# The products with w_in_2 as three fp32r products of rounded and remaining parts, their weights in panels of half a slot

## What is computed

```python
u = modulate(rmsnorm(h, norm_mix_g), shift, scale)      # 512 x 1024
z, xbc, dt_raw, xp, gates = split(u @ w_in_2)           # z 2048, xbc 4096, dt 32, pool 1024, gates 2048 columns
y_ssd  = ssd_branch(z, xbc, dt_raw, ...)                # conv, silu, chunked state-space scan: 8 groups x 4 chunks of 128
y_pool = pool_branch(xp, pool_w, pool_scale)            # window means, a grouped product
h = h + mod * ((y_ssd @ w_br_ssd) * sigmoid(g0) + (y_pool @ w_br_pool) * sigmoid(g1)) @ w_out_2
# then router, 64 experts (top 8), shared expert, final norm
```

## Time and profile before

| | |
|---|---|
| median of 3 runs | 2885.08 us (2883.0 to 2885.61) |
| the profiled execution | 2896.94 us, span 2894.9 us |
| PE busy | 2614.2 us (90%) of the span |
| DVE, ACT, POOL busy | 1111.9, 655.1, 538.1 us |
| mean granted TensorE clock | 0.928 |

### The profile page before, as it was taken

One profiled execution on the slowest core, in us unless ns is written; L12 is line 12 of the kernel. 1 busy time (PEld: TensorE's weight loads), 2 busy tenths in 40 slices (PEclk: granted clock), 3 DMA queues, 4 the chain that ended last, 5 costly groups with the idle time before them and its releaser, 6 DMA issues.

```text
span 2894.9 us, 25467 instructions
## 1 busy us (share of the span) xinstructions
PE 2614.2 (90%) x8938; PEld 1524.9 (53%) x8938; DVE 1111.9 (38%) x2005; ACT 655.1 (23%) x1084; POOL 538.1 (19%) x442
## 2 busy tenths in 40 slices
PE   5999996899999889999998899986889999999995
PEld 3885345678777533445454444574444444444443
DVE  4545333499851332445555321124611111111113
ACT  3334243333332222222222110222111111111111
POOL 2330003234333200000000001130322322222220
PEclk8997678899999899899999799997989999999998
DMA  3222000155632022211112011212089999999995
GB/s 117 75 88 87 1 0 30 58 175 181 214 122 102 0 87 83 66 44 44 56 46 87 30 58 58 87 33 80 31 324 304 343 339 314 353 331 332 324 321 147
DMA packets 163575, 403.43 MB, mean 139 GB/s; under 512 B 12128, under 2 KB 88928, under 8 KB 139552
## 3 DMA queue, kind: packets, MB, share of 16 engines
q1 hardware_dynamic: 142896, 342.27, 33.2%
q0 software_dynamic: 19440, 55.79, 8.0%
q10 hardware_dynamic: 1152, 4.19, 0.4%
HBM read 378.62 MB, written 39.32 MB: 144 GB/s over the span
## 4 chain that ended last, share of the span: by engine, by line
PE 78%; DVE 9%; DMA 7%; issue 2%; ACT 2%; POOL 1%; POOLq 0%; SPq 0%; DVEq 0%; ACTq 0%
PE bank L644 42%; PE bank L653 19%; DMA arena<-u_rows,rows_in 4%; PE bank L811 3%; PE bank L751 2%; PE bank L728 2%; PE bank L1078 2%; PE bank L670 2%; PE bank L918 1%; DVE hn L1594 1%; DMA arena<-in_w_up 1%; PE bank L742 1%; DVE arena L1725 1%; PE bank L732 1%; DVE inv L1591 1%
## 5 line engine op out<-in xcount | busy, mean ns | idle before, releaser
L644 PE MATMUL bank<-arena 128*128 128x512 f32 x1840 | 812.6, 598 | 8.6 <-DVE arena L1940 5.8
L644 PEld LDWEIGHTS bank<-arena 128*128 128x128 f32 x1840 | 348.2, 192 | 421.2 <-issue 417.1
L644 PE MATMUL bank<-hn,arena 128*128 128x512 f32 (+1 forms) x1168 | 530.8, 614 | 13.7 <-ACT hn L1161 10.6
L644 PEld LDWEIGHTS bank<-hn,arena 128*128 128x128 f32 (+1 forms) x1168 | 225.2, 195 | 298.7 <-issue 282.5
L2060 DVE TENSOR_TENSOR arena<-arena,bank 128x256 f32<-128x256 f32 x62 | 26.1, 421 | 501.6 <-ACT arena L1554 501.6
L603 POOL DMA_INDIRECT y_rows<-arena,rows_out x62 | 98.8, 1594 | 504.8 <-DVE arena L2072 271.2
L653 PE MATMUL bank<-x_high,w_high 128*128 128x512 f32 x352 | 141.1, 401 | 14.1 <-DVE x_low L1601 13.0
L560 POOL TENSOR_TENSOR pooled_low<-arena,pooled_high 128x512 fp32r<-128x512 f32 x8 | 9.9, 1266 | 742.8 <-ACT pooled_high L1473 742.8
L653 PE MATMUL bank<-x_low,w_high 128*128 128x512 f32 x352 | 139.7, 397 | 0.0
L653 PE MATMUL bank<-x_high,w_low 128*128 128x512 f32 x352 | 139.7, 397 | 0.0
L2072 DVE TENSOR_SCALAR arena<-bank,arena 128x512 f32<-128x512 f32 x124 | 93.1, 751 | 115.8 <-PE bank L644 115.8
(11 more groups left out here) (307 smaller groups left out, 3919.1 us busy)
## 6 DMA issues: line engine op xcount, KB each, us to landing
arena<-in_we_gate SPq DMA_DIRECT2D x62, 1024.0 KB
arena<-in_we_up SPq DMA_DIRECT2D x62, 1024.0 KB
arena<-in_we_down SPq DMA_DIRECT2D x62, 1024.0 KB, 8.7
arena<-in_w_in SPq DMA_DIRECT2D x30, 1024.0 KB, 5.9
arena<-in_w_ada SPq DMA_DIRECT2D x12, 2048.0 KB, 8.1
arena<-in_w_up SPq DMA_DIRECT2D x22, 1024.0 KB, 11.3
arena<-in_w_in SPq DMA_DIRECT2D x17, 512.0 KB, 4.2
arena<-in_w_out SPq DMA_DIRECT2D x4, 2048.0 KB, 8.1
```

The source lines that it names most:

```text
L644: ins = nc.tensor.matmul(out, w(k), rhs(k), start=first and k == 0, stop=last and k == nk - 1)
```

## The change

Each of the 73 products becomes a `split_product`. ACT makes the activations' high parts straight from the scaled norm (adding the shift), DVE the low parts, for which `hn` no longer holds the shifted sum. Weights come in panels of half a slot (8 x 256 columns): four half-slots in slots 0 and 1, and slot 2 holds the high parts of two panels in turn. Such a panel with its one or two tiles is a unit. ACT rounds unit u+2 as soon as it has read the last product of unit u (`in2_high_part`), POOL subtracts tile by tile into the panel's own place, and PE waits for its tile's low part. The squares of the group norm move from `sq` to another buffer.

```diff
@@ panels
-        x_panel = len(PANELS)
-        for c0, c1, v in ((6144, 6560, 4), (6560, 6944, 7), (6944, 7200, 9)):
-            add_panel(one(w_in2, 0, KD, c0, c1), S("product"), PRODUCTS["x"] + v)
+        def add_half_panel(copies, value):
+            n = len(IN2)
+            IN2.append(add_panel(copies, S("product"), value, NSLOT + n % 4, [latest[n // 2]] if n < 4 else [IN2[n - 4]]))
+        for c0, c1, v in ((6144, 6304, 2), (6304, 6560, 4), (6560, 6816, 6), (6816, 6944, 7), (6944, 7200, 9)):
+            add_half_panel(one(w_in2, 0, KD, c0, c1), PRODUCTS["x"] + v)
...
+        last = {s: [i for i in IN2 if SLOT_OF[i] == NSLOT + s][-1] for s in range(4)}
+        FREED = {0: [last[0], last[1]], 1: [last[2], last[3]], 2: [IN2[-1]]}
...
                 add_panel(one(A["w_br_ssd"], KD * kg, KD * kg + KD, 512 * half, 512 * half + 512),
-                          S("product"), PRODUCTS["ssd_out"] + 2 * half + kg + 1)
+                          S("product"), PRODUCTS["ssd_out"] + n + 1, n % NSLOT, FREED[n] if n < NSLOT else None)
@@ POOL
+            for j, (u, i) in enumerate(IN2_TILES):
+                pool_eng.wait_ge(S("w_high"), W_UNITS["in2"] + u + 1)
+                pool_eng.tensor_tensor(in2_tile(j, "low"), in2_tile(j, "whole"), in2_tile(j, "high").bitcast(f32),
+                                       ALU.subtract).then_inc(S("w_low"), 1)
@@ PE
+            def in2_product(j, out, ready=None):
+                pe.wait_ge(S("w_low"), W_LOW["in2"] + j + 1)
+                high, low = in2_tile(j, "high"), in2_tile(j, "low")
+                split_product(out, lambda k: high[:, k, :], lambda k: low[:, k, :], lambda k: in2_x[k][:, :],
+                              lambda k: x_low[:, k, :], ready).then_inc(S("product"), 1)
@@ ACT
-            shifted("n4", 0)
+            def in2_high_part(u):
+                panel_here(act, IN2[IN2_UNITS[u][0]])
+                if u >= 2:
+                    act.wait_ge(S("product"), IN2_DONE[u - 2])
+                nc.scalar.activation(in2_part(u, "high"), in2_part(u, "whole"), ACT.Copy).then_inc(S("w_high"), 1)
+            act.wait_ge(S("product"), PRODUCTS["ple"] + 2 * KD)
+            in2_high_part(0)
+            in2_high_part(1)
+            for k in range(KD):
+                act.wait_ge(S("norm_mul"), KD if k == KD - 1 else k + 1)
+                nc.scalar.activation(in2_x[k][:, :], hn[:, k, :], ACT.Identity, bias=mod[:, k:k + 1]).then_inc(S("x_high"), 1)
...
@@ ACT, read_tile of the SSD stage
                                          scale=0.5).then_inc(S("z_tanh"), 1)
+                    if j == 1:
+                        in2_high_part(SSD_UNIT + i // 2 + 2)
                     return
...
                                      bias=col("conv_b2", ch)).then_inc(S("s_tap3"), 1)
+                if j in (3, 5):
+                    in2_high_part(SSD_UNIT + i // 2 + 2)
                 if waiting:
                     xbc_silu()
@@ DVE
             modulated("n4", col("norm_mix", 0, KD), KD)
+            for k in range(KD):
+                dve.wait_ge(S("x_high"), 4 * KD + k + 1)
+                nc.vector.scalar_tensor_tensor(x_low[:, k, :], hn[:, k, :], mod[:, k:k + 1], in2_x[k][:, :].bitcast(f32),
+                                               ALU.add, ALU.subtract).then_inc(S("x_low"), 1)
```

More of the change, by code:

```diff
@@ L178, in two_blocks @@
         ssd["th"] = sq[:, 2:4, :]
-        late = lay(dtk["end"], gs=(16, T), tmp=(2, T))
+        late = lay(dtk["end"], gs=(16, T), tmp=(2, T), y_sq=(4, T))
+        Y_SQ, Y_INV = late["y_sq"], sq[:, 2:4, :]
+        late["end"] = dtk["end"] + 18 * T
+        in2_x = [rounded(f"in2_x{k}", [P, T], at) for k, at in enumerate(
+            [shp_at + 4 * SHAPES[name][0] for name in ("dist", "causal", "chunked")] +
+            [sq_at, sq_at + 4 * T, arena_at + 4 * ssd["end"], inv_at + 4 * T, inv_at])]
         wo_x_high = rounded("wo_x_high", [P, KD, T], arena_at + 4 * RING)
@@ L240, in two_blocks @@
         SLOT_OF, BEFORE, latest = [], [], [-1] * NSLOT
+        HALF = PANEL // 2
+        SLOT_AT = [s * PANEL for s in range(NSLOT)] + [s * HALF for s in range(4)]
         def slot(i, w):
-            v = arena[:, SLOT_OF[i] * PANEL:SLOT_OF[i] * PANEL + KD * w]
+            v = arena[:, SLOT_AT[SLOT_OF[i]]:SLOT_AT[SLOT_OF[i]] + KD * w]
             return v.rearrange("p (k n) -> p k n", n=w)
@@ L247, in rows, with add_panel @@
             return W[k0 * P:k1 * P, c0:c1].rearrange("(k p) n -> p k n", p=P)
-        def add_panel(copies, semaphore, value, chosen=None):
+        def add_panel(copies, semaphore, value, chosen=None, after=None):
             i = len(PANELS)
@@ L253, in add_panel @@
             SLOT_OF.append(s)
-            BEFORE.append(latest[s])
-            latest[s] = i
+            BEFORE.append([latest[s]] if after is None else after)
+            if s < NSLOT:
+                latest[s] = i
             PANELS.append(([(slot(i, w)[:, 0:b - a, d0:d0 + c1 - c0], rows(W, a, b, c0, c1))
@@ L338, in two_blocks @@
-        gts_panel = len(PANELS)
-        for q in range(4):
-            add_panel(one(w_in2, 0, KD, 7200 + 512 * q, 7712 + 512 * q), S("product"), PRODUCTS["gates"] + 4 * q + 4)
+        IN2 = []
+        def add_half_panel(copies, value):
[3 more added lines that the diff above has]
+            add_half_panel(one(w_in2, 0, KD, c0, c1), PRODUCTS["x"] + v)
@@ new lines, in two_blocks @@
+        for q in range(8):
+            add_half_panel(one(w_in2, 0, KD, 7200 + 256 * q, 7456 + 256 * q), PRODUCTS["gates"] + 2 * q + 2)
+        IN2_UNITS = [(0, 160, [(0, SH), (SH, P)]), (1, 256, [(0, P), (P, P)]), (2, 256, [(0, P), (P, P)]), (3, 128, [(0, P)]),
+                     (4, 256, [(0, P), (P, P)])] + [(n, 256, [(0, P), (P, P)]) for n in range(6, 6 + 3 * SG + 8)]
+        IN2_TILES = [(u, i) for u, unit in enumerate(IN2_UNITS) for i in range(len(unit[2]))]
+        IN2_DONE = [PRODUCTS["x"] + v for v in (2, 4, 6, 7, 9)] + [PRODUCTS["ssd"] + 2 * n + 2 for n in range(3 * SG)] + \
+                   [PRODUCTS["gates"] + 2 * n + 2 for n in range(8)]
@@ L358, in two_blocks, with in2_part, in2_tile @@
             ARRIVED.append(counted[SLOT_OF[i]])
-        W_UNITS, _ = places([("z", len(Z_PANELS)), ("wo", 4), ("up", FT), ("down", 12), ("ple", 4), ("pool_out", 4),
-                             ("wo2", 4)])
+        W_UNITS, _ = places([("z", len(Z_PANELS)), ("wo", 4), ("up", FT), ("down", 12), ("ple", 4), ("in2", len(IN2_UNITS)),
+                             ("pool_out", 4), ("wo2", 4)])
         W_UNITS = {name: first for name, (first, _) in W_UNITS.items()}
+        W_LOW, _ = places([("z", len(Z_PANELS)), ("wo", 4), ("up", FT), ("down", 12), ("ple", 4), ("in2", len(IN2_TILES)),
+                           ("pool_out", 4), ("wo2", 4)])
+        W_LOW = {name: first for name, (first, _) in W_LOW.items()}
+        def in2_part(u, of):
+            n, width, _ = IN2_UNITS[u]
+            if of == "whole":
+                return slot(IN2[n], width)
+            at = SLOT_AT[SLOT_OF[IN2[n]]]
+            v = in2_high[:, u % 2, :] if of == "high" else w_low_flat[:, at:at + HALF]
+            return v[:, 0:KD * width].rearrange("p (k n) -> p k n", n=width)
+        def in2_tile(j, of):
+            u, i = IN2_TILES[j]
+            c, width = IN2_UNITS[u][2][i]
+            return in2_part(u, of)[:, :, c:c + width]
         def up_columns(pair, parts):
@@ L451, in _ @@
             for i, (copies, _, _) in enumerate(PANELS):
-                if BEFORE[i] >= 0:
-                    sp.wait_ge(PANELS[BEFORE[i]][1], PANELS[BEFORE[i]][2])
+                for j in BEFORE[i]:
+                    if j >= 0:
+                        sp.wait_ge(PANELS[j][1], PANELS[j][2])
                 for dst, src in copies:
@@ L770, in _ @@
             for t in range(KD):
-                pe.wait_ge(S("w_low"), W_UNITS["wo"] + t // 2 + 1)
+                pe.wait_ge(S("w_low"), W_LOW["wo"] + t // 2 + 1)
                 if t >= 7:
@@ L788, in _ @@
                 pair = i // 2
-                pe.wait_ge(S("w_low"), W_UNITS["up"] + pair + 1)
+                pe.wait_ge(S("w_low"), W_LOW["up"] + pair + 1)
                 if i >= 6:
@@ L799, in _ @@
             for j, (pn, k0, k1, t0) in enumerate(DOWN_UNITS):
-                pe.wait_ge(S("w_low"), W_UNITS["down"] + j + 1)
+                pe.wait_ge(S("w_low"), W_LOW["down"] + j + 1)
                 for t in (t0, t0 + 1):
@@ L822, in _ @@
                 panel_here(pe, proj_panel)
-                pe.wait_ge(S("w_low"), W_UNITS["ple"] + t // 2 + 1)
+                pe.wait_ge(S("w_low"), W_LOW["ple"] + t // 2 + 1)
                 if t >= 3:
@@ L978, in _ @@
             for t in range(KD):
-                pe.wait_ge(S("w_low"), W_UNITS["wo2"] + t // 2 + 1)
+                pe.wait_ge(S("w_low"), W_LOW["wo2"] + t // 2 + 1)
                 if t >= 7:
```

84 lines of the change are left out of this document (33 added, 51 removed).

## The result

| | before | after |
|---|---|---|
| median, us | 2884.04 (2878.25 to 2885.61, 4 runs) | 2846.4 (2839.74 to 2858.58, 4 runs) |
| profiled execution, us | 2896.94 | 2839.74 |
| its span, us | 2894.9 | 2837.9 |

The ratio of the times is 0.9882, 95% interval 0.9857 to 0.9908. The forecast was 2848.0, range 2812 to 2872. A second series of the changed kernel gave 2850.46 and a ratio of 0.9891 (0.9851 to 0.9931).

A forecast was written before the change was run, and what follows sets the result against it. PE, busy 90% of the span, was taken as the bound. Terms summed to -37.1 us: 2859.8 from the profiled 2896.94, or 2848.0 after allowing for that execution being 11.9 above the median; range 2812 to 2872.

The forecast's parts named there:

- The hold of DVE by POOL: DVE operations with two SBUF inputs wait for POOL's subtraction to end; +4.3 us at each group boundary.
- full-gain rival: DVE gets through POOL's work or the waits fall elsewhere: 2792 us; chance of ending under 2825: 0.17.
- start of the x stage: Behind norm n4, POOL delays DVE's multiplications, so PE starts the x stage later: +5.6 us.
- wait for the exponential: Behind the x stage, a rounding stands ahead of the ACT exponential PE waits for: +2.0 us, stall 4.6.
- clock behind it: After the 4.6 us stall behind the x stage, clock 0.5 for some 6.6 us, half lost: +3.2 us.
- first six products with their boundary: First six SSD products save 7.7 us, the first group boundary adds 4.3: -3.4 us.
- boundary: End of each SSD group: POOL's subtractions delay both L1832, PE waits directly; +4.3 us for each of 8.
- stall of the second chunk: In each SSD group's second chunk, DVE's chain ends at Q + 11.3 and PE waits 2.8 us.
- clock's relief of 7 us: At SSD boundaries longer stalls make the clock fall before PE resumes, leaving less low clock: 0.9 us each, -7.
- seven groups: SSD groups of six products: -8.1 saved, +2.8 second chunk, +4.3 boundary, -1.0 each; -7.0 us before clock relief.
- The clock loss by the stall in the second chunk: Rival: each 2.8 us stall lowers the clock, +23 us, without relief: 2878; chance of 2866 to 2879: 0.13.
- Slower for want of low parts: Rival: PE waits for low parts in every unit; 2940 if POOL takes 11 us a unit; chance 0.03.

The follow-up runs named there:

- e1: Changed kernel with POOL writing zeros where it subtracted the weights' remainders, all other instructions and waits kept: 2802.45 us, 0.9729 of the kernel before.
- e1b: Changed kernel with POOL multiplying one SBUF operand by 2^-12 in place of the two-operand subtraction: 2811.49 us, 0.9776 of the kernel before.
- e3: Changed kernel with a group's last half panel rounded only after the next group's first exponential: 2821.48 us, 0.9792 of the kernel before.
- e7: Changed kernel with each POOL subtraction as two instructions of half the elements: 2826.42 us, 0.9796 of the kernel before.
- e6: e5 plus the rounding after tile 3 behind ACT's tanh and the second unit's rounding behind the x parts: 2800.17 us, 0.9712 of the kernel before.
- e5: e3's move plus the x half panel rounded one tile later, against the changed kernel: 2800.78 us, 0.9700 of the kernel before.
- e10: The kernel before, unchanged, profiled once more: one execution of 2886.15 us.
- e9: The changed kernel again, nothing altered: 2850.46 us, 0.9891 of the kernel before.
- e2: Changed kernel with all preparation kept but products back to two-pass fp32, reading the remainders: 2987.34 us, 1.0372 of the kernel before.

## Why the prediction was right

The saving on PE, its price in waits for DVE and the places of these waits were as predicted; one term, the clock's, was wrong, and smaller errors offset it.

**Bound and saving.** PE's pace was as the rows said. The gates are the plain case, two products on the chain of the kernel after (against 13.73 in the earlier trace rows):
```profile
1613.89 11.10 PE bank L704 x48
...
1690.81 11.12 PE bank L704 x48
```
0.231 us a MATMUL against the 0.233 used; gates -22.3 against -20.5 forecast. By the four passes of the Trainium skill ("FP8 and Floating Point Precision", TensorE Precision Notes), three for four, two products would have taken an estimated 10.3 us; the trace doesn't agree. ACT and POOL stayed hidden there, as walked.

**The hold of DVE by POOL** was the mechanism on which the forecast differed from a full gain, and e1, e1b, e3 and e7 show it. With the holds off the chain (e1, e6) the stages lose 89 us. The 93 of the saving are nearly all there, and e5 and e6 come within 9 us of the full-gain rival's 2792. The Trainium skill ("SBUF — State Buffer", Who interferes with whom) speaks of a GpSimd instruction that reads SBUF, whatever the number of its operands; here the ones with a single SBUF operand held DVE for 0.3 us in a boundary (e1b), the subtractions with two for 3.75.

**Term by term** (forecast, measured in the profiles):
- start of the x stage +5.6, +4.6; its products -11.5, -12.7; wait for the exponential +2.0, +1.8; clock behind it +3.2, and the stretch up to the SSD stage took 2.5 more. Together -0.7, -3.8.
- first six products with their boundary -3.4, -4.1.
- boundary +4.3 each, +3.8: xbc ended 8.3 us after the last product (1385.05 - 1376.73), not 8.9.
- stall of the second chunk 2.8, 1.8: DVE's chain ended 10.3 us behind the fill products (1352.87 - 1342.53), not 11.3.
- gates -20.5, -22.3; w_br_ssd +1.5, +0.6: PE's wait went from 5.82 to 6.42 us and has DMA's landing of 7.90 us at its end, so the first panel did not share with the two queued behind it. Last group 0, +0.7.

**The step that failed is the clock's relief of 7 us.** Stretches of 12 us behind two restarts of PE, the kernel after, then e1 (whose stall is 3.5 us as before); columns as in the earlier trace rows:
```profile
1385.10:1397.10 12.00, 12.00 (x39) 9.76 (x40) 5.93 (x13) 1.94 (x4) 0.00 (x0) 0.62 0.00 1
1445.00:1457.00 12.00, 12.00 (x43) 9.84 (x44) 6.38 (x14) 2.32 (x4) 0.00 (x0) 0.70 0.00 0
```
```profile
1358.85:1370.85 12.00, 12.00 (x44) 9.71 (x45) 6.45 (x14) 2.32 (x4) 0.00 (x0) 0.72 0.00 1
1412.08:1424.08 12.00, 12.00 (x39) 9.77 (x40) 5.93 (x13) 1.86 (x4) 0.00 (x0) 0.61 0.00 1
```
Over the seven the mean is 0.69 in both, with a stall of 7.3 or of 3.5 us, and 0.73 in the kernel before. The clock does fall ahead of PE's restart (1385.10 here), as the prediction said:
```profile
1380.00:1382.00 2.00, 0.00 (x0) 0.00 (x0) 2.00 (x1) 0.55 (x1) 2.00 (x2) 0.63 0.74 252
...
1390.30:1392.30 2.00, 2.00 (x6) 1.58 (x5) 1.21 (x2) 0.59 (x1) 0.00 (x0) 0.50 0.00 0
```
But it is still at 0.50, 1.2 GHz, 5 to 7 us behind the restart, where the earlier trace rows had 0.65. With the longer stall the low stretch began earlier, but it did not end earlier. So instead of -7 the sum should have had (0.73 - 0.69) x 12 x 7 = +3 us. The whole groups say the same: PE worked at 1.2 GHz for 46.0 us of the seven before and for 51.5 after, and half of the difference is 2.8 us. In e1 it was 52.9, so the 3 us are not the longer stall's; e1 has the shorter one and the three fp32r products. What in them keeps the clock low for longer is open.

The seven groups came out at -14.3, against -7.0 forecast and some 6 of the relief, -13 in all. That agreement is luck, from errors that cancel: a group's time without its stalls fell by 7.6 us (61.13 - 3.5 to 59.10 - 7.3 - 1.8), not by 8.1 and a relief of 0.9; and the two stalls together were 10 us shorter over the seven than walked.

**The total.** That the median came within 2 us of the 2848.0 is luck in part. The stages fell by 43.3 us (43.0 between e10 and e9), the sum said 37.1, and the medians fell by 37.6 and 32.5. The 6 to 10 us between stages and medians are not in the changed stages. The profiles of e10 and e9 differ by 41.0 us in span, 43.0 less in the stages and 0.9 more in the expert stage. What is left is within what the expert stage scatters; whether it is a little longer after the change stays open.

**The rivals.** The clock loss by the stall in the second chunk did not come (stalls of 1.8 us). Slower for want of low parts: PE never waited for w_low of these products in the changed kernel, and e2 puts the whole cost side at 46 us against a saving of 89, so no slower outcome was near. The price that the prediction gave this rival, 43 us when POOL takes 9.7 us for a unit, doesn't come out of its own numbers. It leaves POOL 8.5 us (11.2 less 2.7) for a whole unit, but PE waits tile by tile and roundings run a unit ahead, so by the code POOL would bind only when a unit took it more than PE's 11.2 us; it took 5.1. No run tried that.

## What to carry to other kernels

Work handed to an idle GpSimd (POOL) was free here only where VectorE (DVE) was idle too or had an input in PSUM: a subtraction of two SBUF operands stopped each two-SBUF-input operation of VectorE that came beside it, and that mattered at the few places where PE waits for VectorE. Find these on the chain and release GpSimd's work elsewhere; here two moved calls (e5) gave 46 us more, 2801 against 2846. Where it can't be moved, cut it into shorter instructions, which shortens the hold (some 20 us here, e7).

## What the runs showed of the hardware that was not expected

- A GpSimd instruction that reads one SBUF operand of 1024 columns and takes 2.8 us hardly holds VectorE (1.64 us for a pair of two-SBUF-input operations, 1.35 alone); a subtraction that reads two and takes 2.5 us holds it to its end (5.10).
- After PE's restart the low clock lasted as long behind a stall of 7.3 us as behind one of 3.5 (mean 0.69 of full over 12 us in both), and zeros in a third of the products did not shorten it.
- The same stalls taken away saved 10.2 us in one kernel and 15.7 in another, since PE's time at 1.2 GHz moved by +6.4 us in the one and by -5.7 in the other.
